# A hybrid attention, mLSTM and ConvFFN block on eight cores: weights stored block by block in the order of use, and the attention steps in bursts between whole projection groups

## The reference, cut to what matters

```python
h    = rmsnorm(x, norm_mix_g)
proj = h @ w_in                      # 2048 x 6664: attention q, k, v (12 heads of 128),
                                     # mLSTM q, k, v, o-gate (4 heads of 128), 8 gate columns
attn = dilated_attention(q, k, v)    # q and k: rmsnorm per head, rotary; three branches with
                                     # dilations 1, 4, 16, merged by their softmax denominators
hm   = rmsnorm(mlstm(...) * sigmoid(o_gate))
x    = x + concat(attn, hm) @ w_out  # 2048 x 2048
h2   = rmsnorm(x, norm_ffn_g)
u    = causal_dwconv(h2 @ w_up)      # 2048 x 11264, 3 taps
gate, val = split(u)
x    = x + (silu(gate) * val) @ w_down   # 5632 x 2048
```

## Time and profile before

| | us |
|---|---|
| median of 3 runs | 3430.94 |
| lowest, highest | 3417.77, 3591.8 |
| the profiled execution (one of these runs) | 3430.94 |
| its span, slowest core (core 4) | 3429.9 |
| spans of the 8 cores | 3396.6 to 3429.9 |

### The profile page before, as it was taken

The page is one execution under the profiler, slowest core; times in us unless marked ns, Lnnn a source line. Parts: engine busy times, 40 slices in busy tenths (PEclk is TensorE's granted clock), DMA queues, the critical chain, the costliest instruction groups (busy, mean ns, idle before and its releaser), DMA issues.

```text
span 3429.9 us, 43524 instructions; the slowest of 8 cores (3396.6 to 3429.9 us)
## 1 busy us (share of the span) xinstructions
PE 3151.9 (92%) x16124; PEld 1479.8 (43%) x16124; DVE 1493.1 (44%) x2088; ACT 1023.4 (30%) x1602; POOL 173.5 (5%) x152
## 2 busy tenths in 40 slices
PE   4786888799999987989999999899989999999999
PEld 2432444344444443434444444344434444444444
DVE  3454444355555541114666666300046666663000
ACT  2244644355555552333222222100012222221000
POOL 0000000000000000000000000000000000000000
PEclk8898999999999998999999999999999999999999
DMA  9231233432233127898777787788775666555786
GB/s 210 55 44 25 36 62 59 91 61 49 47 61 61 35 56 201 171 177 100 78 77 74 79 80 78 121 122 134 121 98 79 81 81 80 75 74 89 121 137 115
DMA packets 440177, 308.12 MB, mean 90 GB/s; under 512 B 19744, under 2 KB 406816, under 8 KB 439840
## 3 DMA queue, kind: packets, MB, share of 16 engines
q0 software_dynamic: 321984, 174.99, 42.9%
q1 hardware_dynamic: 117984, 130.34, 14.7%
HBM read 427.85 MB, written 52.43 MB: 140 GB/s over the span
## 4 chain that ended last, share of the span: by engine, by line
PE 75%; DMA 9%; DVE 8%; ACT 5%; issue 3%; DVEq 0%; SPq 0%; ACTq 0%; POOL 0%; POOLq 0%
PE ps L981 36%; PE ps L1022 15%; PE ps L698 7%; PE ps L927 4%; DVE mem L709 3%; PE ps L508 3%; DMA wslot<-w_down 3%; DMA x1d<-mem 2%; DVE mem L442 2%; DMA mem<-xT 2%; PE ps L494 1%; PE ps L716 1%; DMA mixd<-mem 1%; PE ps L384 1%; PE ps L789 1%
## 5 line engine op out<-in xcount | busy, mean ns | idle before, releaser
L981 PE MATMUL ps<-mem,wslot 128*128 128x512 bf16 x5632 | 1218.8, 380 | 10.9 <-DMA wslot<-w_up 10.9
L981 PEld LDWEIGHTS ps<-mem,wslot 128*128 128x128 bf16 x5632 | 551.7, 98 | 677.7 <-issue 15.0
L1022 PE MATMUL ps<-mem,wslot 128*128 128x512 bf16 x2816 | 611.9, 380 | 16.9 <-DMA wslot<-w_down 16.8
L999 DVE SCALAR_TENSOR_TENSOR mem<-mem,cfs 128x1024 f32<-128x1024 f32 x352 | 452.1, 1284 | 288.5 <-ACT mem L996 203.4
L996 ACT ACTIVATE mem<-mem,cfs 128x1024 f32<-128x1024 f32 x176 | 217.0, 1233 | 787.1 <-DVE mem L988 787.1
L1022 PEld LDWEIGHTS ps<-mem,wslot 128*128 128x128 bf16 x2816 | 275.8, 98 | 352.7 <-issue 23.7
L698 PE MATMUL ps<-mem,wslot 128*128 128x512 bf16 x1536 | 382.9, 380 | 0.7 <-ACT mem L513 0.7
L988 DVE TENSOR_TENSOR mem<-ps,mem 128x512 f32<-128x512 f32 x352 | 242.9, 690 | 140.6 <-PE ps L981 120.6
L1031 DVE TENSOR_TENSOR mem<-ps,mem 128x512 f32<-128x512 f32 x64 | 44.3, 692 | 577.9 <-PE ps L1022 527.3
L927 PE MATMUL ps<-mem,wslot 128*128 128x512 bf16 x1024 | 238.9, 388 | 10.3 <-DMA mem<-mixd 10.3
L698 PEld LDWEIGHTS ps<-mem,wslot 128*128 128x128 bf16 x1536 | 150.0, 99 | 173.7 <-issue 35.0
(11 more groups left out here) (117 smaller groups left out, 2267.2 us busy)
## 6 DMA issues: line engine op xcount, KB each, us to landing
wslot<-w_up POOLq DMA_DIRECT2D x88, 1024.0 KB, 16.5
wslot<-w_down POOLq DMA_DIRECT2D x32, 1408.0 KB, 15.9
mem<-xT SPq DMA_DIRECT2D x8, 2048.0 KB, 21.0
mem<-xT SPq DMA_DIRECT2D x64, 256.0 KB, 8.4
x1d<-mem SPq DMA_DIRECT2D x64, 256.0 KB, 5.3
mem<-x1d SPq DMA_DIRECT2D x64, 256.0 KB, 7.7
outT<-mem SPq DMA_DIRECT2D x64, 256.0 KB, 3.9
wslot<-w_in POOLq DMA_DIRECT2D x6, 2048.0 KB, 19.9
```

Of the source, the lines that this page charges most:

```text
L981: K.mm([lambda e, kc=kc: e.matmul(ps[bi][:], sl[:, kc, c0:c0 + 128], h2p[:, kc, t2 * TT:(t2 + 1) * TT], start=(kc == 0), stop=(kc == KC - ...
L999: K.op(dve, lambda e, k=k: e.scalar_tensor_tensor(out=a, in0=y[:, k:k + HS], scalar=wc(k), in1=a, op0=ALU.mult, op1=ALU.add), [B_yy, B_cf, ...
L1022: K.mm([lambda e, k=k: e.matmul(ps[bi][:], slv[:, k, jc2 * 128:(jc2 + 1) * 128], actT[:, kh * 22 + k, t2 * TT:(t2 + 1) * TT], start=(kh == ...
```

## The change

Two things change together.

**Weights.** The host packs the four matrices into `wa` (39 blocks of 128 x 8192 float32) and `wb` (16 blocks of 128 x 5632), in the order and layout in which the slots hold them. A block load reads one row of 32 KB (22 KB for w_down) per partition, in one transfer; the first block is cut into four transfers with rows of 8 KB. The bytes, the slots and the order are as before. The 8 gate columns have a small array of their own.

**Attention.** The stream is replaced by a loop over whole groups. After the 16 matmuls of group g, the norm and rotary of group g-1 are issued, then 2 or 3 attention steps of the head before (`pace`), in one burst. Groups come as four q tiles and then four k tiles. Head 0 has no attention steps beside its projections; all 18 steps of head 11 come after the last projection. The rotary is computed otherwise: ACT squares the bank and copies it, scaled by the norm's gain, to `qg` (bf16); PE only permutes (`psgn`); DVE does two multiplies, an add and the last multiply, in float32, where before it did two multiplies on the bank (L709), PE added them (L716, L717) and DVE did the last multiply (L726). For q the reordering by residues (r) moves from the moving operand of the three matmuls to the last DVE multiply. The S banks, the PV banks and a lag of two steps stay; in the drain head 11 has four S banks, two PV pairs and a lag of three.

```diff
-    blocks = []
     wv = lambda s: s[:].rearrange("p (k n) -> p k n", n=512)
-    for c0 in (5632, 4608, 5120, 6144, 3072, 3584, 4096):
-            ...
-            blocks.append([(wv, w_in_v[:, :, c0:c0 + 512])])
-    ...
+    blocks = [(wa[i], 8192) for i in range(17)]
     for hf in range(2):
-        ...
+        blocks += [(wa[17 + i], 8192) for i in range(22)] + [(wb[i], 5632) for i in range(16)]
...
-        K.dma(pool, [vf(wslots[sl]) for vf, src in blocks[i]], [src for vf, src in blocks[i]], B_ws[sl], True)
+        src, n = blocks[i]
+        cuts = range(0, n, n // 4 if i == 0 else n)
+        w = n // len(cuts)
+        K.dma(pool, [wslots[sl][:, c:c + w] for c in cuts], [src[:, c:c + w] for c in cuts], B_ws[sl], True)
...
     def proj_group(h, sl, B_slot, part, tt):
...
-        for kc in range(KC):
-            ins = pe.e.matmul(bank[:], sl[:, kc, c0:c0 + 128], hT[:, kc, tsl], start=(kc == 0), stop=(kc == KC - 1))
-            if kc < KC - 1:
-                clk["mm"] += 1
-                yield
...
+        bank, B_bank = dense(2, [... for kc in range(KC)], [B_slot] + hTt(tt))
...
         K.op(act, lambda e: e.activation(out=sc["sq"], in_=bank[:], func=AF.Square), [B_bank], [sc["B_sq"]])
-        for nm, tab in (("a", cos2), ("b", sin2)):
-            K.op(dve, lambda e: e.scalar_tensor_tensor(out=sc[nm], in0=bank[:], scalar=cf[:, gcol:gcol + 1],
-                                                       in1=tab[:, tsl], op0=ALU.mult, op1=ALU.mult),
-                 [B_bank, B_cf, B_cs], [sc["B_" + nm]])
-        mov = (lambda x: x.rearrange("p (s r) -> p r s", r=4)) if part == 0 else (lambda x: x)
+        K.op(act, lambda e: e.activation(out=sc["qg"], in_=bank[:], func=AF.Copy, scale=cf[:, gcol:gcol + 1]),
+             [B_bank, B_cf], [sc["B_qg"]])
 
         def stage2():
-            K.mm([lambda e: e.matmul(ps[2][:], ones, mov(sc["sq"]), start=True, stop=True)], [sc["B_sq"], B_one], [B_ps[2]])
-            K.mm([lambda e: e.matmul(ps[3][:], ident, mov(sc["a"]), start=True, stop=False),
-                  lambda e: e.matmul(ps[3][:], psgn, mov(sc["b"]), start=False, stop=True)],
-                 [sc["B_a"], sc["B_b"], B_cb], [B_ps[3]])
+            K.mm([lambda e: e.matmul(ps[2][:], ones, sc["sq"], start=True, stop=True)], [sc["B_sq"], B_one], [B_ps[2]])
+            K.mm([lambda e: e.matmul(ps[3][:], psgn, sc["qg"], start=True, stop=True)], [sc["B_qg"], B_cb], [B_ps[3]])
...
-        def stage3():
-            K.op(dve, lambda e: e.tensor_tensor(out=dst[:, tsl], in0=ps[3][:], in1=sc["rs"], op=ALU.mult),
-                 [B_ps[3], sc["B_rs"]], [B_dst])
-        later(7, stage2)
-        later(14, stage3)
...
+            K.op(dve, lambda e: e.tensor_tensor(out=sc["t2"], in0=ps[3][:], in1=sin2[:, tsl], op=ALU.mult),
+                 [B_ps[3], B_cs], [sc["B_t2"]])
+            K.op(dve, lambda e: e.tensor_tensor(out=sc["t1"], in0=sc["qg"], in1=cos2[:, tsl], op=ALU.mult),
+                 [sc["B_qg"], B_cs], [sc["B_t1"]])
+            K.op(dve, lambda e: e.tensor_tensor(out=sc["t1"], in0=sc["t1"], in1=sc["t2"], op=ALU.add),
+                 [sc["B_t1"], sc["B_t2"]], [sc["B_t1"]])
+            if part == 0:
+                rs_ = lambda a: a.rearrange("p (s r) -> p r s", r=4)
+                K.op(dve, lambda e: e.tensor_tensor(out=dst[:, tsl].rearrange("p (r s) -> p r s", r=4), in0=rs_(sc["t1"]),
+                                                    in1=rs_(sc["rs"]), op=ALU.mult), [sc["B_t1"], sc["B_rs"]], [B_dst])
+            else:
+                K.op(dve, lambda e: e.tensor_tensor(out=dst[:, tsl], in0=sc["t1"], in1=sc["rs"], op=ALU.mult),
+                     [sc["B_t1"], sc["B_rs"]], [B_dst])
+        return stage2
...
     v_load(0)
+    pace = (3, 2, 2, 2, 3, 2, 3, 3)
+    prev2 = None
+    steps_ = iter(())
     for h in range(NHA):
...
         for g in range(8):
-            for _ in proj_group(h, sl, B_slot, 1 - g % 2, g // 2):
-                run_due()
-                if items and items[0][0] <= clk["mm"]:
-                    step(items.pop(0)[1])
+            st2_ = proj_group(h, sl, B_slot, g // 4, g % 4)
+            if prev2 is not None:
+                prev2()
+            prev2 = st2_
+            for _ in range(pace[g]):
+                next(steps_, None)
+        for _ in steps_:
+            pass
         if h % 2 == 1:
             w_issue()
+        if h < NHA - 1:
+            steps_ = attn_head(h, [(6, 7)], [4, 5], 2)
+    prev2()
...
-    while items or pend or due:
-        ...
+    for _ in attn_head(NHA - 1, [(6, 7), (0, 1)], [4, 5, 2, 3], 3, mix_load):
+        pass
```

More of the change, by code:

```diff
@@ L189, in build @@
     xT = nc.dram_tensor("xT", [D, S], F32, kind="ExternalInput").ap()
[L190 to L193, removed]
+    wa = nc.dram_tensor("wa", [39, P, 8192], F32, kind="ExternalInput").ap()
+    wb = nc.dram_tensor("wb", [16, P, 5632], F32, kind="ExternalInput").ap()
+    w_g = nc.dram_tensor("w_g", [D, 8], F32, kind="ExternalInput").ap()
     cbd = nc.dram_tensor("cb", [P, NCB], F32, kind="ExternalInput").ap()
@@ L658, in build @@
     o += 2048
-    NPT = 8
-    ptb, B_pt = zip(*[alloc(o + i * 1024, TT, BF16, "pt%d" % i) for i in range(NPT)])
+    ptb, B_pt = zip(*[alloc(o + i * 1024, TT, BF16, "pt%d" % i) for i in range(4)])
     vd_nat = vd.rearrange("(b p) d -> p b d", p=P)
@@ L759, in attn_tile @@
         return banks
-    pend = []
-    st = {"hold": 0, "drain": False}
-    LAG = 2
-    sbs = [4, 5]
-    ready = []
-    def attn_s(h, T, first, last, bk):
-        hb = h % 2
-        (c0, smm, mask, pvl, dview, kb) = bk
-        si = sbs[rot["S"] % len(sbs)]
-        rot["S"] += 1
-        pi = rot["pt"] % NPT
-        rot["pt"] += 1
-        Sb, B_S = ps[si], B_ps[si]
-        pt, B_p = ptb[pi], B_pt[pi]
-        K.mm([lambda e, a=a: e.matmul(Sb[:, a[0] * 128:(a[0] + 1) * 128], a[1], a[2], start=True, stop=True)
-              for a in smm], [B_qT[hb][T]] + kb, [B_S])
-        K.op(act, lambda e: e.activation(out=pt[:, c0:TT], in_=Sb[:, c0:TT], func=AF.Exp), [B_S], [B_p])
-        K.op(dve, lambda e: e.tensor_tensor(out=pt[:, c0:TT], in0=pt[:, c0:TT], in1=mask[:, c0:TT], op=ALU.mult),
-             [B_p, B_cb], [B_p])
-        pend.append((h, T, first, last, bk, pt, B_p))
@@ L805, in fin @@
                 note(mix_tok[T], K.dma(sp, mixd[h * 128:(h + 1) * 128, t0:t0 + TT], ostb[oi], B_ost[oi], False))
-                if h == NHA - 1:
-                    ready.append(T)
-            later(6, fin)
-            st["hold"] = 0 if st["drain"] and T == NT - 2 else 2
-    def step(item):
-        if item is not None:
-            attn_s(*item)
-        if st["hold"]:
-            st["hold"] -= 1
-        if st["hold"]:
-            return
-        n = 1 if len(pend) <= LAG + 1 else 2
-        while pend and n and (len(pend) > LAG or item is None) and not st["hold"]:
-            attn_pv(pend.pop(0))
-            n -= 1
-    items = []
-    for h in range(NHA):
-        j = 0
-        for T in range(NT):
-            bl = attn_tile(h, T)
-            for k, bk in enumerate(bl):
-                items.append((h * 128 + 76 + j * 128 / 18, (h, T, k == 0, k == len(bl) - 1, bk)))
-                j += 1
+                if on_tile is not None:
+                    on_tile(T)
+        for (T, first, last, bk) in allb:
+            (c0, smm, mask, pvl, dview, kb) = bk
+            si = sbs[rot["S"] % len(sbs)]
+            rot["S"] += 1
+            pi = rot["pt"] % 4
+            rot["pt"] += 1
+            Sb, B_S = ps[si], B_ps[si]
+            pt, B_p = ptb[pi], B_pt[pi]
+            K.mm([lambda e, a=a: e.matmul(Sb[:, a[0] * 128:(a[0] + 1) * 128], a[1], a[2], start=True, stop=True)
+                  for a in smm], [B_qT[hb][T]] + kb, [B_S])
+            K.op(act, lambda e: e.activation(out=pt[:, c0:TT], in_=Sb[:, c0:TT], func=AF.Exp), [B_S], [B_p])
+            K.op(dve, lambda e: e.tensor_tensor(out=pt[:, c0:TT], in0=pt[:, c0:TT], in1=mask[:, c0:TT], op=ALU.mult),
+                 [B_p, B_cb], [B_p])
+            pend.append((T, first, last, bk, pt, B_p))
+            if len(pend) > lag:
+                do_pv(pend.pop(0))
+            yield
+        while pend:
+            do_pv(pend.pop(0))
+            yield
     v_load(0)
+    pace = (3, 2, 2, 2, 3, 2, 3, 3)
+    prev2 = None
+    steps_ = iter(())
     for h in range(NHA):
@@ L1088, in _params, with _pack @@
     return cfn
+def _pack(w_in, w_out, w_up, w_down):
+    r3 = lambda w: w.reshape(-1, P, w.shape[1]).transpose(1, 0, 2)
+    wi, wo, wu, wd = r3(w_in), r3(w_out), r3(w_up), r3(w_down)
+    wa = np.empty((39, P, KC, 512), np.float32)
+    for i, c in enumerate((5632, 4608, 5120, 6144, 3072, 3584, 4096)):
+        wa[i] = wi[:, :, c:c + 512]
+    for i in range(6):
+        wa[7 + i, :, :, :256] = wi[:, :, i * 256:(i + 1) * 256]
+        wa[7 + i, :, :, 256:] = wi[:, :, 1536 + i * 256:1536 + (i + 1) * 256]
+    for i in range(4):
+        wa[13 + i] = wo[:, :, i * 512:(i + 1) * 512]
+    for i in range(22):
```

(6 more changed lines are left out.)

117 lines of the change are left out of this document (38 added, 79 removed).

## The result

| | before | after |
|---|---|---|
| runs compared, us | 3417.77 to 3430.94 | 3468.32 to 3473.04 |
| profiled execution, us | 3430.94 | 3468.32 |
| its span, slowest core | 3429.9 (core 4) | 3467.3 (core 3) |

The change made the kernel slower by 1.3%: ratio 1.0134, 95% interval 1.0101 to 1.0168. The forecast of 3401 us went the other way, by 67 us against the profiled execution. Runs in which the cores of a die showed a lower granted clock are left out of all comparisons here, which leaves two runs of a2_steps_first and one of a3_warm.

What follows compares the result with a forecast made beforehand. The prediction took PE to bound the kernel, three quarters of the span. From 3430.9 us it added 6.5 for attention and 0 for the drain and took off 36 for the weights: 3401, range 3350 to 3480.

Steps and rivals of the forecast that it cites:

- The walk of a burst: Attention: following PE, ACT and DVE through eight bursts gave 27.4 us, with projections 55.0 us a head against 52.0.
- The strided last multiply: Attention, q groups: DVE's last multiply reads with a stride, taken at 1.31 us, with 0.69 as the other bound.
- The clock: Rival, attention: PE falls to half clock in four long bursts a head, 63 us, time 3464; chance 0.18.
- Head 0: Attention's first head, projections alone: 31.0 us plus some 5 us waiting for the cos/sin table, 36 in all.
- Drain: After the last projection: set by transfers, so taken as 0 us change, bounds -5 to +12.
- Weights, FFN: FFN turns between up and down: long rows remove 26 of 27.7 us of PE waits for weights.
- Weights, start and w_out: Start and output projection: long rows save 4 us at the start and 6 of 15.6 us of waits in w_out.
- long rows hold back SP: Rival, start, w_out and drain: SP's rows wait behind 32 KB weight rows, 74 us, time 3485; chance 0.07.
- the likeliest case: Whole kernel: attention and weights terms both as summed, 3401 us, own range 3375 to 3435; chance 0.42.

Runs made afterwards that it cites:

- a2_steps_first: a1_bursts with one order turned round: in a burst, attention steps issued ahead of the norm and rotary of the group before; 3386.9 and 3397.9 us.
- a3_warm: a1_bursts with eight filler matmuls, computing nothing used, in each of the two waits at the turn of a head; 3442.6 us.
- w1_long_rows: The kernel before with only the weights packed in long rows (32 and 22 KB), its attention kept; ratio 1.001, 3430.2 to 3435.5 us.
- a1_bursts: The kernel before with only the new attention loop, weights and loads as before; ratio 1.0097, 3451.7 to 3467.1 us.
- m2_both: a2_steps_first with long rows for the FFN's weights alone; ratio 0.9928 to the kernel before, 3391.2 to 3406.4 us.
- n1_after_steps_first: The changed kernel with one edit: attention steps of a burst issued ahead of the epilogue of the group before; ratio 0.9976, 3407.2 to 3429.9 us.
- a2_again: The same kernel as a2_steps_first, timed in more rounds; ratio 0.9927, 3389.3 to 3408.5 us.
- n2_mix: n1_after_steps_first with POOL's first weights waiting for the first 2 MB of x, and five blocks around w_out in 2 KB rows; ratio 0.9882.

## Why the prediction was wrong, point by point

- *The walk of a burst* held. After's eight bursts sum to 27.96 us (27.4 forecast), with 27.6 of projections and 1.69 of half clock 57.25, what the head shows. The strided last multiply takes 1.09 us, inside the bounds 0.69 and 1.31. The walk named the queueing on ACT but took the order of issue as given; a2_steps_first shows it was the lever, worth 6 us a head.
- *The clock* is the step that failed in attention. The prediction put it at nothing, since no single wait of the walk was over 2.6 us, and one wait of 2.54 had left the clock. The waits were 2.48 and 2.55, as walked, and the clock fell behind 60 of 80 turns. A single row could not carry that bound: waits alike to 0.01 us are followed by either clock. That is the step's error; what decides the clock there stays open. The rival's mechanism was right, its price (63 us) too high: 18.2 us by a3_warm. It let all four long bursts of a head do it; the two others, whose waits come in pieces of at most 1.4 us, show no group at half clock. Adding the 18.2 to the sum, 11 heads of 0.6 us of walk error, and the longer wait for cos/sin (w1_long_rows: attention +4) accounts for the stage: on the median core 6.5 + 18.2 + 6.6 + 4, some 35 us, measured 36.2.
- *Head 0* took 43.2 us (653.9 to 697.1) instead of 36. Most of it is the cos/sin table: in the chain of after its wait is 20.26 us (14.01 before), in that of a1_bursts, beside short rows, 17.38; in that of w1_long_rows, with the attention of before, 21.33. What PE runs on meanwhile was not measured by itself.
- *Drain*: right in size (66.0 us on the slowest core from the last projection to the point where the table begins w_out, 65.8 before), but by luck. From the last projection matmul to the first of w_out the median core takes 32.5 us, 32.7 before: the new attention alone makes it 36.9 (a1_bursts), the long rows alone 29.5 (w1_long_rows), and the two cancel. Both lie within the forecast's bounds; its 0 rested on neither.
- *Weights, FFN*: right, -22 on the median core (-34.5 on the slowest, whose FFN before was the longest of all), where I took -26.
- *Weights, start and w_out*: the step that failed. I took -4 and -6; they came to +14 and +6 (median core). The rival "long rows hold back SP" named the mechanism and both places; its price was 74 us, w1_long_rows shows 15 at the start, 13 in w_out and 4 at the table, 32. I gave it 0.07 because weights had kept their rate beside 16 KB rows of cos/sin. That row has the roles reversed, long rows on SP and short ones on the weights' side, and for only 6 us. It could not speak for short rows of SP beside 32 KB rows. By place, w1_long_rows has 15 of the rival's 21 us at the start and 13 of its 42 in w_out; the drain, priced at 10.6, got shorter.
- The range held the time (3350 to 3480), since these rivals had been kept in it; the likeliest case was wrong in sign.

## What to carry to other kernels

Before spreading or bunching work, write down the order in which each engine gets its operations: an epilogue that nobody waits for soon, issued ahead of a step's Exp and mask, cost 6 us a head here, and swapping the two lines gained it back. Use long rows for a stream that has the DMA engines to itself, and short rows, or a later issue, where another queue's small rows are needed soon. Before the clock's price is put at nothing, look at many waits of that length: one that left the clock is no bound.

## What was not expected of the hardware

- PE's clock fell behind 60 of 80 turns with two waits of 2.48 to 2.70 and 2.55 us, and stayed at full speed behind 20, with the same waits; a single wait of 2.54 had left it in before. In 45 of the 60 the group between the waits ran at full speed (3.62 us).
- Long DMA rows (8 KB and 32 KB) in one queue slowed another queue's 1 KB rows: a 2 MB tile of x landed at 15.9 us without weights beside it, at 20.3 beside rows of 2 KB, and at 26.6 to 27.3 beside the long ones.
- In m2_both and n1_after_steps_first two neighbouring cores ran the first three or four heads at a granted clock of 0.81, the groups of 16 alike at 4.38 us. Core 3 of n1_after_steps_first, busy time by stretch:

```profile
690.00:715.00 25.00, 23.08 (x100) 10.00 (x99) 13.54 (x22) 13.59 (x23) 0.00 (x0) 0.81 0.00 1
790.00:815.00 25.00, 23.62 (x143) 12.15 (x141) 16.40 (x26) 16.56 (x29) 0.00 (x0) 0.81 0.04 12
840.00:865.00 25.00, 23.35 (x155) 12.67 (x154) 17.11 (x26) 16.45 (x29) 0.00 (x0) 0.94 0.03 11
```

  Core 1 of the same execution shows 1.00 in the first two stretches. It cost these cores some 20 us. In a2_again, n2_mix and a3_warm no core's attention is longer than the others' by more than 10 us; what sets it off stays open.
